# A decoder trunk on one core: weight units loaded, rounded and split in two halves, the low part written over the raw words

## Chip, core and metric

The kernel runs on one core of one Trainium2 chip. Its time is the device time of the whole program, in microseconds (us). The core has a matrix engine (TensorE, PE), whose weight loads stand in a lane of their own (PEld), and VectorE (DVE), ScalarE (ACT), GpSimd (POOL) and SyncE (SP). SP here does little but issue the loads of the weights.

## What is computed

A decoder trunk of two layers on 512 tokens of width 1024, everything in fp32. Cut to what matters, the reference is:

```python
def swiglu(x, w_gate_up, w_down):
    gate, up = jnp.split(x @ w_gate_up, 2, axis=-1)
    return (jax.nn.silu(gate) * up) @ w_down

for l in range(DEPTH):                                   # DEPTH = 2
    h = h + 0.5 * swiglu(rmsnorm(h, ffn1_norm[l]), ffn1_w_gate_up[l], ffn1_w_down[l])
    u = rmsnorm(h, mix_norm[l])
    # layer 0: gated DeltaNet, layer 1: forgetting attention; both beside attention into 256 memory tokens
    h = h + jnp.concatenate([main, mem_out], axis=-1) @ w_out[l]
    h = h + 0.5 * swiglu(rmsnorm(h, ffn2_norm[l]), ffn2_w_gate_up[l], ffn2_w_down[l])
    # after layer 0: shared keys and values from rmsnorm(h) @ kv_w
return rmsnorm(h, final_norm)
```

The hidden width of the feed-forward is 2816, so the four feed-forward blocks hold most of the multiplications.

## The kernel before

**Units.** All weights pass through 189 units. A full unit is 2048 fp32 words for each of the 128 partitions (1 MB): 8 blocks along the contracted dimension by 256 output columns. A unit of a down projection is 1408 words (11 blocks of 128 columns, 704 KB), two of them to one output tile; two units, the first ones of the gdnin and kv phases, have 1024 words. Unit u uses slot u % 2, and a slot holds three tiles: `raw` (as loaded), `w_hi` (rounded to fp32r) and `w_lo` (raw minus w_hi, rounded).

**Steps of a unit.** SP loads `raw` with two DMAs (`load`, line 380, issued at line 383). ACT writes `w_hi` (`round_hi`, line 873, at line 880). DVE writes `w_lo` (`cut_lo`, line 1214, at line 1219). PE then makes three products for each block, hi by x_hi, hi by x_lo and lo by x_hi (`split_products`, lines 464 to 466), so a full unit has 48 matmuls and a down unit 33.

**Waits.** A load of unit u waits until `w_lo` of unit u-2 is cut (semaphore `lo_ready`), which is when `raw` is no longer read. `round_hi` of unit u waits for the load and for `unit_done` of unit u-2, which is when PE has left `w_hi` and `w_lo`. PE waits for `w_lo` of its whole unit (line 472 in `unit`, line 490 in `down_tile`).

**Order on the engines.** Each engine runs its own written order, phase by phase: memtr, xtr, memkv (4 short units of 256 tokens), memvtr, up0, down0, gdnin0, gdn0, wout0, up1, down1, kv0, up2, down2, foxin0, fox0, wout1, up3, down3, final. In an up phase a step is, on ACT: `round_hi` two units ahead, Silu (line 976), then after POOL's product (line 1714) `hid_hi` (line 980); on DVE: the scaled copy out of PSUM (line 1248), `cut_lo` two units ahead, `hid_lo` (line 1359). The second unit of the next down phase waits for the last `hid_lo`. In a down phase step m is, on ACT: `round_hi` of units 2m+2 and 2m+3 of the phase, `feed_hi` (x_hi of the next phase, line 883), a square (line 895); on DVE: `cut_lo(2m+2)`, the update of h (line 1375), `feed_lo` (x_lo, line 1225), `cut_lo(2m+3)`; on POOL: one addition of the square into `square_sum` (line 1695). The units of step m+1 are the ones that `cut_lo` makes in step m. The last step of a down phase so makes the first two units of the next phase. Steps 0 to 5 of the 8 run in a hardware loop, the last two stand by themselves. In down3, the last one, `feed_hi` and `feed_lo` are left out, and DVE makes y_t from h alone.

In gdnin0 and kv0 the first unit has only 24 matmuls, and takes x_hi and x_lo block by block as they come. After it PE sums the squares over the partitions (line 505), for the root mean square of ACT.

Of the kernel before, what the change touches and what calls it, by code (L numbers as in the profile page):

```python
# [2 lines left out]

# [25 lines left out]
P = 128  # L29
# [20 lines left out]
HALF = NP // 2  # L50
FULL_UNIT = KT * 2 * P
DOWN_UNIT = HALF * P
ROW_B = 32


# [42 lines left out]
def build_trunk(nc, mem, x, ffn1_norm, ffn1_gu, ffn1_down, mix_norm, ffn2_norm, ffn2_gu, ffn2_down,  # L98
# [21 lines left out]
    with ExitStack() as ctx:  # L120
# [53 lines left out]
        for s in range(2):  # L174
            slot_at.append(cursor[0])
            raw.append(place(f"raw{s}", [P, FULL_UNIT]))
            w_hi.append(place(f"w_hi{s}", [P, FULL_UNIT], F32R))
            w_lo.append(place(f"w_lo{s}", [P, FULL_UNIT], F32R))
        x_at, X_BYTES = cursor[0], 2 * KT * SEQ * 4
        x_hi = place("x_hi", [P, KT, SEQ], F32R)  # L180
        x_lo = place("x_lo", [P, KT, SEQ], F32R)
# [115 lines left out]
        raw_in = [sem(f"raw_in{s}") for s in range(2)]  # L297
# [71 lines left out]
        def weights_landed(u0, i=0):  # L369

            return 32 * (u0 // 2 + 1) + 32 * i

        block = ctx.enter_context(nc.Block())


        @block.sync
        def _(sp):
            def load(u0, parts, i=0):

                if u0 >= 2:  # L380
                    sp.wait_ge(lo_ready, u0 - 1 + 2 * i)
                for dst, src in parts:
                    sp.dma_start(dst, src).then_inc(raw_in[slot(u0)], 16)

            def load_cols(u0, w, col, i=0, width=2 * P):
                dst = raw[slot(u0)][:, 0:KT * width].rearrange("p (k n) -> p k n", k=KT)
                half = KT // 2
                load(u0, [(dst[:, a:a + half, :], w[:, a:a + half, bass.ds(col, width)])
                          for a in (0, half)], i)

            def load_gate_up(u0, w, n, i=0):
                dst = raw[slot(u0)][:].rearrange("p (k g n) -> p k g n", k=KT, g=2)
                load(u0, [(dst[:, :, g, :], w[:, :, bass.ds(g * FFN + n, P)]) for g in (0, 1)], i)

            def load_down(u0, w, half, n, i=0):
                dst = raw[slot(u0)][:, 0:DOWN_UNIT].rearrange("p (k n) -> p k n", k=HALF)
                cut = HALF // 2
                load(u0, [(dst[:, a:b, :], w[:, half * HALF + a:half * HALF + b, bass.ds(n, P)])
                          for a, b in ((0, cut), (cut, HALF))], i)

            for name in phases:
                kind, idx = name[:-1], int(name[-1])
                u = first_unit[name]
                if kind == "memtr":
                    sp.dma_start(mem_tok[:], mem_rows).then_inc(mem_in, 16)
                elif kind == "memkv":
                    if idx == 0:
                        sp.wait_ge(x_in, 16 * TT)
                    for n in range(2):
                        load_cols(u + n, blocks(mem_w_kv[idx]), n * MEM_WIDTH)  # L410
                elif kind == "up":
                    for n in range(2):
                        load_gate_up(u + n, ffn_gu[idx], n * P)
                    with sp.Fori(0, NP // 2 - 1) as i:
                        for j in range(2):
                            load_gate_up(u + 2 + j, ffn_gu[idx], (2 * i + (2 + j)) * P, i)
                elif kind == "down":
                    with sp.Fori(0, KT) as m:
                        for half in range(2):
                            load_down(u + half, ffn_down[idx], half, m * P, m)  # L420
                elif kind == "gdnin":
                    w = blocks(gdn_w_in[0])
                    dst = raw[slot(u)][:, 0:KT * P].rearrange("p (k n) -> p k n", k=KT)
                    a_col = 4 * WIDTH
                    load(u, [(dst[:, :, 0:ROW_B], w[:, :, a_col:a_col + ROW_B]),
                             (dst[:, :, ROW_B:P], w[:, :, a_col + HEADS:a_col + HEADS + P - ROW_B])])
                    for n in range(12):
                        load_cols(u + 1 + n, w, n * 2 * P)
                    load_cols(u + 13, w, 4 * WIDTH + 2 * HEADS)
                elif kind == "foxin":  # L430
                    for n in range(4):
                        load_cols(u + n, blocks(fox_w_in[0]), n * 2 * P)
                elif kind == "wout":
                    for n in range(KT // 2):
                        if idx == 0 and n == 1:
                            sp.wait_ge(w_prod, TT)
                        load_cols(u + n, blocks(w_out[idx]), n * 2 * P)
                elif kind == "kv":
                    w = blocks(kv_w)
                    dst = raw[slot(u)][:, 0:KT * P].rearrange("p (k n) -> p k n", k=KT)  # L440
                    load(u, [(dst[:, :, 0:HEADS], w[:, :, 2 * WIDTH:2 * WIDTH + HEADS]),
                             (dst[:, :, HEADS:P], w[:, :, 0:P - HEADS])])
# [10 lines left out]
        def _(pe):  # L453
# [14 lines left out]
            def unit(u0, g0, xh, xl, i=0, outs=2, tokens=SEQ, feed=None, ready=x_ready, release=False,  # L468
                     order=range(KT)):

                s, width = slot(u0), outs * P
# [1398 lines left out]
```

## Time and profile before

| | |
|---|---|
| median of 3 runs | 2218.85 us (2218.21 to 2219.61) |
| span of the profiled execution | 2218.7 us |
| PE busy | 2129.1 us, 96% of the span |
| PEld busy | 1743.8 us, 79% |
| DVE busy | 932.8 us, 42% |
| ACT busy | 842.6 us, 38% |
| POOL busy | 429.7 us, 19% |
| DMA | 188.64 MB, 85 GB/s over the span |
| mean granted TensorE clock | 0.979 |

The time of the profiled execution outside its span is not shown apart; the span lies 0.15 us under the median of the unprofiled runs. Busy time of PE counts matmuls from start to modelled end, and these overlap: one 128x512 matmul is shown with 390 ns while the next starts 226 ns after it. So a full unit takes 10.87 us of PE and a down unit 7.48 us at full clock.

### The profile page before, as it was taken

How to read it: one execution, taken by the hardware profiler on the slowest of the kernel's cores; microseconds unless marked ns; L12 is line 12 of the kernel's file. 1: busy time of each engine (PE TensorE's matmuls, PEld its weight loads, DVE VectorE, ACT ScalarE, POOL GpSimd, SP SyncE). 2: the span in 40 equal slices, each digit the busy share in tenths (PEclk: the TensorE clock that was granted, in tenths of full speed). 3: DMA queues.
4: the chain of work that ended last, by engine and by line, in shares of the span. 5: the costliest groups of instructions: out<-in, count | busy, mean ns of one | idle time of the engine just before them, and what ended most of it. 6: DMA issues, size and time to landing. Idle time of an engine off the chain costs nothing.

```text
span 2218.7 us, 25639 instructions
## 1 busy us (share of the span) xinstructions
PE 2129.1 (96%) x9944; PEld 1743.8 (79%) x9944; DVE 932.8 (42%) x864; ACT 842.6 (38%) x939; POOL 429.7 (19%) x288
## 2 busy tenths in 40 slices
PE   6999999999989989999999999999999899999998
PEld 5788888877758878888888888888887478888886
DVE  6433333465442335333333443333434545333333
ACT  4333332367533434344322334432222544344221
POOL 3121210223132612212211011221110012212211
PEclk8999999999999999999999999999998999999999
DMA  4333323322100013433233443332334003333232
GB/s 153 107 100 96 95 71 99 106 76 85 49 1 1 1 53 84 111 95 95 77 102 96 143 124 95 95 95 84 91 109 152 1 22 110 97 95 95 78 93 75
DMA packets 319222, 188.64 MB, mean 85 GB/s; under 512 B 10537, under 2 KB 316858, under 8 KB 318906
## 3 DMA queue, kind: packets, MB, share of 16 engines
q1 hardware_dynamic: 317168, 179.33, 28.2%
q10 hardware_dynamic: 1130, 5.32, 0.6%
q0 software_dynamic: 864, 3.15, 0.3%
q8 instruction: 43, 0.70, 0.1%
q14 instruction: 17, 0.14, 0.0%
HBM read 182.53 MB, written 5.24 MB: 85 GB/s over the span
## 4 chain that ended last, share of the span: by engine, by line
PE 60%; DVE 1%; ACT 1%; issue 0%; ACTq 0%; POOL 0%; DVEq 0%; POOLq 0%
PE ps L464 19%; PE ps L466 19%; PE ps L465 19%; PE ps L849 1%; PE ps L515 0%; PE ps L830 0%; PE ps L541 0%; DVE f_stat L1647 0%; DVE fp L1643 0%; PE ps L818 0%; PE ps L532 0%; PE ps L839 0%; DVE w_lo L1219 0%; ACT bias_ts L1180 0%; PE ps L505 0%
## 5 line engine op out<-in xcount | busy, mean ns | idle before, releaser
L464 PE MATMUL ps<-x_hi,w_hi 128*128 128x512 f32 x1920 | 755.8, 394 | 15.3 <-DVE w_lo L1219 8.6
L465 PE MATMUL ps<-x_lo,w_hi 128*128 128x512 f32 x1920 | 750.1, 391 | 0.0
L466 PE MATMUL ps<-x_hi,w_lo 128*128 128x512 f32 x1920 | 750.1, 391 | 0.0
L880 ACT ACTIVATE w_hi<-raw 128x2048 fp32r<-128x2048 f32 (+2 forms) x189 | 326.3, 1726 | 786.8 <-PE ps L466 755.5
L1219 DVE TENSOR_TENSOR w_lo<-raw,w_hi 128x2048 fp32r<-128x2048 f32 (+2 forms) x189 | 414.4, 2192 | 227.6 <-ACT w_hi L880 227.2
L464 PEld LDWEIGHTS ps<-x_hi,w_hi 128*128 128x128 f32 x1920 | 362.6, 189 | 99.0 <-DVE w_lo L1219 10.8
L465 PEld LDWEIGHTS ps<-x_lo,w_hi 128*128 128x128 f32 x1920 | 362.6, 189 | 77.2 <-issue 1.9
L466 PEld LDWEIGHTS ps<-x_hi,w_lo 128*128 128x128 f32 x1920 | 362.1, 189 | 75.5
L1714 POOL TENSOR_TENSOR gate_up<-gate_up 128x512 f32<-128x512 f32 x88 | 194.5, 2210 | 795.8 <-ACT gate_up L976 795.8
L466 PE MATMUL ps<-hid_hi,w_lo 128*128 128x512 f32 x704 | 273.9, 389 | 0.0
L464 PE MATMUL ps<-hid_hi,w_hi 128*128 128x512 f32 x704 | 273.9, 389 | 0.0
L465 PE MATMUL ps<-hid_lo,w_hi 128*128 128x512 f32 x704 | 273.9, 389 | 0.0
L1248 DVE TENSOR_TENSOR gate_up<-ps,rstd 128x1024 f32<-128x1024 f32 x88 | 107.8, 1225 | 326.8 <-PE ps L466 326.2
L1695 POOL TENSOR_TENSOR square_sum<-square_sum,gate_up 128x512 f32<-128x512 f32 (+1 forms) x64 | 94.4, 1475 | 529.4 <-ACT gate_up L895 483.2
L464 PEld LDWEIGHTS ps<-hid_hi,w_hi 128*128 128x128 f32 x704 | 132.1, 188 | 27.7
L466 PEld LDWEIGHTS ps<-hid_hi,w_lo 128*128 128x128 f32 x704 | 132.1, 188 | 27.4
L465 PEld LDWEIGHTS ps<-hid_lo,w_hi 128*128 128x128 f32 x704 | 132.1, 188 | 27.2
L1359 DVE TENSOR_TENSOR hid_lo<-gate_up,hid_hi 128x512 f32 (+1 forms) x88 | 60.9, 693 | 180.7 <-ACT hid_hi L980 180.7
L980 ACT ACTIVATE hid_hi<-gate_up 128x512 f32 (+1 forms) x88 | 55.8, 634 | 212.0 <-POOL gate_up L1714 212.0
L1375 DVE SCALAR_TENSOR_TENSOR h<-ps,h 128x512 f32 (+1 forms) x32 | 22.1, 692 | 152.0 <-PE ps L466 152.0
L1225 DVE SCALAR_TENSOR_TENSOR x_lo<-h,gains,x_hi 128x512 fp32r<-128x512 f32 (+1 forms) x56 | 44.1, 810 | 38.9 <-ACT x_hi L883 38.9
L895 ACT ACTIVATE gate_up<-h 128x512 f32<-128x512 f32 (+1 forms) x56 | 33.8, 617 | 66.1 <-DVE h L1572 52.2
(256 smaller groups left out, 1570.6 us busy)
## 6 DMA issues: line engine op xcount, KB each, us to landing
raw<-in_ffn_w_gate_up SPq DMA_DIRECT2D x176, 512.0 KB, 4.9
raw<-in_ffn_w_down SPq DMA_DIRECT2D x64, 384.0 KB, 3.9
raw<-in_ffn_w_down SPq DMA_DIRECT2D x64, 320.0 KB, 3.2
raw<-in_gdn_w_in SPq DMA_DIRECT2D x26, 512.0 KB, 4.6
raw<-in_w_out SPq DMA_DIRECT2D x16, 512.0 KB, 4.4
raw<-in_kv_w SPq DMA_DIRECT2D x12, 512.0 KB, 5.0
raw<-in_mem_w_kv SPq DMA_DIRECT2D x8, 512.0 KB, 4.8
raw<-in_fox_w_in SPq DMA_DIRECT2D x8, 512.0 KB, 4.1
```

Source lines behind the costliest of these rows:

```text
L464: nc.tensor.matmul(dst, hi, xh, start=first, stop=False)
L465: nc.tensor.matmul(dst, hi, xl, start=False, stop=False)
L466: return nc.tensor.matmul(dst, lo, xh, start=False, stop=last)
L880: nc.scalar.activation(w_hi[s][:, 0:n], raw[s][:, 0:n], ACT.Copy).then_inc(hi_ready, 1)
L895: nc.scalar.activation(gate_up[:, b, 0, 0:tokens], src, ACT.Square).then_inc(sq_ready, 1)
L980: nc.scalar.activation(hid_hi[:, bass.ds(at, 1), :], gate_up[:, j, 0:1, :], ACT.Copy).then_inc(hid_hi_ready, 1)
L1219: nc.vector.tensor_tensor(w_lo[s][:, 0:n], raw[s][:, 0:n], w_hi[s][:, 0:n].bitcast(F32), ALU.subtract).then_inc(lo_ready, 1)
L1225: nc.vector.scalar_tensor_tensor(dst, src, gain, hi.bitcast(F32), op0=ALU.mult, op1=ALU.subtract).then_inc(x_ready, 1)
L1248: nc.vector.tensor_tensor(dst, src, by, ALU.mult).then_inc(evac, 1)
L1359: nc.vector.tensor_tensor(hid_lo[:, bass.ds(at, 1), :], gate_up[:, j, 0:1, :], hid_hi[:, bass.ds(at, 1), :].bitcast(F32), ALU.subtract).th ...
L1695: nc.gpsimd.tensor_tensor(square_sum[:, 0:tokens], square_sum[:, 0:tokens], gate_up[:, b, 0, 0:tokens], ALU.add).then_inc(sum_ready, 1)
L1714: nc.gpsimd.tensor_tensor(gate_up[:, j, 0, :], gate_up[:, j, 0, :], gate_up[:, j, 1, :], ALU.mult).then_inc(prod_ready, 1)
```

## The change

A unit is handled in two halves, from the load to the matmuls, and `w_lo` lies at the address of `raw`: DVE writes the difference over its own input. The half is cut at 1024 words: blocks 0 to 3 and 4 to 7 of a full unit, blocks 0 to 7 and 8 to 10 of a down unit. A load now needs what PE reads to be free: the first half of unit u waits for `half_used` of unit u-2, which PE raises with the ninth of the 16 (in a down unit: of the 11) split products of that unit; the second half waits for `unit_done` of unit u-2. Four DMAs load a unit instead of two (256 KB each in a full unit; 256, 256, 64 and 128 KB in a down unit). ACT and DVE have two instructions per unit instead of one, and ACT's wait for `unit_done` is gone. PE waits for the first half at the start of a unit, and for the second in the middle. The loads of the two narrow units spread over the whole tile. An SBUF area of 8192 bytes per partition stays as padding, so that the tiles of the other phases lie as before.

```diff
+            w_lo.append(place(f"w_lo{s}", [P, FULL_UNIT], F32R, at=slot_at[s]))
             w_hi.append(place(f"w_hi{s}", [P, FULL_UNIT], F32R))
-            w_lo.append(place(f"w_lo{s}", [P, FULL_UNIT], F32R))
+        cursor[0] += 8192
...
-            def load(u0, parts, i=0):
+            def load(u0, half, parts, i=0):
                 if u0 >= 2:
-                    sp.wait_ge(lo_ready, u0 - 1 + 2 * i)
+                    sp.wait_ge((half_used, unit_done)[half], u0 - 1 + 2 * i)
                 for dst, src in parts:
-                    sp.dma_start(dst, src).then_inc(raw_in[slot(u0)], 16)
+                    sp.dma_start(dst, src).then_inc(raw_in[slot(u0)][half], 16)
...
+                for half, cuts in enumerate(((0, 4, DOWN_CUT), (DOWN_CUT, DOWN_CUT + 1, HALF))):
+                    load(u0, half, [(dst[:, a:b, :], w[:, part * HALF + a:part * HALF + b, bass.ds(n, P)])
+                                    for a, b in zip(cuts, cuts[1:])], i)
...
             def unit(...)
-                pe.wait_ge(lo_ready, u0 + 1 + 2 * i)
+                pe.wait_ge(lo_ready, 2 * u0 + (1 if order == range(KT) else 2) + 4 * i)
                 for i_c, c in enumerate(order):
+                    if i_c == KT // 2 and order == range(KT):
+                        pe.wait_ge(lo_ready, 2 * u0 + 2 + 4 * i)
...
+                        if (c, o) == (KT // 2, 0):
+                            last.then_inc(half_used, 1)
...
             def down_tile(...)
-                    pe.wait_ge(lo_ready, u0 + half + 1 + 4 * i)
+                    pe.wait_ge(lo_ready, 2 * (u0 + half) + 1 + 8 * i)
+                        if c == DOWN_CUT:
+                            pe.wait_ge(lo_ready, 2 * (u0 + half) + 2 + 8 * i)
+                        if c == DOWN_CUT:
+                            last.then_inc(half_used, 1)
...
             def round_hi(u, i=0):
-                    act.wait_ge(raw_in[s], weights_landed(u, i))
-                    if u >= 2:
-                        act.wait_ge(unit_done, u - 1 + 2 * i)
-                    nc.scalar.activation(w_hi[s][:, 0:n], raw[s][:, 0:n], ACT.Copy).then_inc(hi_ready, 1)
+                    for half in range(2):
+                        act.wait_ge(raw_in[s][half], weights_landed(u, i))
+                        nc.scalar.activation(half_of(w_hi[s], n, half), half_of(raw[s], n, half),
+                                             ACT.Copy).then_inc(hi_ready, 1)
...
             def cut_lo(u, i=0):
-                    dve.wait_ge(hi_ready, u + 1 + 2 * i)
-                    nc.vector.tensor_tensor(w_lo[s][:, 0:n], raw[s][:, 0:n],
-                                            w_hi[s][:, 0:n].bitcast(F32), ALU.subtract).then_inc(lo_ready, 1)
+                    for half in range(2):
+                        dve.wait_ge(hi_ready, 2 * u + half + 1 + 4 * i)
+                        nc.vector.tensor_tensor(half_of(w_lo[s], n, half), half_of(raw[s], n, half),
+                                                half_of(w_hi[s], n, half).bitcast(F32),
+                                                ALU.subtract).then_inc(lo_ready, 1)
```

## Rows read from the trace of the kernel before

**Rows 1.** The page, its first part: engine, busy us, share of span, instructions.
```profile
PE 2129.1 (96%) x9944; PEld 1743.8 (79%) x9944; DVE 932.8 (42%) x864; ACT 842.6 (38%) x939; POOL 429.7 (19%) x288
```

**Rows 2.** Waits of PE: line, waited for, us in total, times, longest us.
```profile
PE ps L464 <- DVE w_lo L1219: 8.6, 4, 4.1
...
PE ps L612 <- POOL sq L1763: 2.4, 3, 0.8
```

**Rows 3.** Lines 880 and 1219 by themselves: count, duration ns min/median/max, forms.
```profile
L880 ACT ACTIVATE w_hi<-raw x189: 1060/1915/1921, 18.3 to 2188.4; 128x2048 fp32r<-128x2048 f32 x123, 128x1408 fp32r<-128x1408 f32 x64, 128x1024 fp32r<-128x1024 f32 x2
...
L1219 DVE TENSOR_TENSOR w_lo<-raw,w_hi x189: 1226/2292/3383, 20.3 to 2189.9; 128x2048 fp32r<-128x2048 f32 x123, 128x1408 fp32r<-128x1408 f32 x64, 128x1024 fp32r<-128x1024 f32 x2
```

**Rows 4.** The page, DMA issues: count, KB each, median us from issue to landing.
```profile
raw<-in_ffn_w_down SPq DMA_DIRECT2D x64, 384.0 KB, 3.9
raw<-in_ffn_w_down SPq DMA_DIRECT2D x64, 320.0 KB, 3.2
...
raw<-in_kv_w SPq DMA_DIRECT2D x12, 512.0 KB, 5.0
...
raw<-in_kv_w SPq DMA_DIRECT2D x1, 24.0 KB, 2.3
```

**Rows 5.** Timeline, one looped tile of down1: start us, duration us, what.
```profile
1150.72 0.39 PE L464 MATMUL ps<-hid_hi,w_hi 128*128 128x512 f32 x1
...
1150.92 1.38 ACT L880 ACTIVATE w_hi<-raw 128x1408 fp32r<-128x1408 f32 x1 [6.10 <-PE ps L466]
1152.21 0.70 ACT L883 ACTIVATE x_hi<-h,gains  x1
...
1153.60 1.39 POOL L1695 TENSOR_TENSOR square_sum<-square_sum,gate_up 128x512 f32<-128x512 f32 x1 [13.56 <-ACT gate_up L895]
...
1153.76 2.71 DVE L1219 TENSOR_TENSOR w_lo<-raw,w_hi 128x1408 fp32r<-128x1408 f32 x1
...
1158.20 0.39 PE L464 MATMUL ps<-hid_hi,w_hi 128*128 128x512 f32 x1
```

**Rows 6.** Timeline, step 6 of down0, outside the loop; below, the looped steps.
```profile
417.26 2.79 POOL L1695 TENSOR_TENSOR square_sum<-square_sum,gate_up 128x512 f32<-128x512 f32 x1 [13.64 <-ACT gate_up L895]
...
417.29 1.61 DVE L1219 TENSOR_TENSOR w_lo<-raw,w_hi 128x1408 fp32r<-128x1408 f32 x1
...
L1219 DVE TENSOR_TENSOR w_lo<-raw,w_hi x12: 1624/2170/2718, 318.7 to 402.4; 128x1408 fp32r<-128x1408 f32 x12
```

The last row is line 1219 by itself in the six looped steps of down0, with its columns as in rows 3.

**Rows 7.** Timeline, the end of down1 and the start of kv0.
```profile
1225.53 0.39 PE L464 MATMUL ps<-x_hi,w_hi 128*128 128x512 f32 x1
...
1227.61 0.70 ACT L883 ACTIVATE x_hi<-h,gains 128x512 fp32r<-128x512 f32 x1
...
1229.01 3.38 DVE L1219 TENSOR_TENSOR w_lo<-raw,w_hi 128x2048 fp32r<-128x2048 f32 x1
...
1232.45 0.50 PE L464 MATMUL ps<-x_hi,w_hi 128*128 128x512 f32 x1 [0.47 <-DVE w_lo L1219]
```

**Rows 8.** Timeline in gdnin0 at the start of its unit 3, and the window 462:464.
```profile
462.44 0.80 PE L464 MATMUL ps<-x_hi,w_hi 128*128 128x512 f32 x1 [4.13 <-DVE w_lo L1219]
...
467.30 0.63 PE L466 MATMUL ps<-x_hi,w_lo 128*128 128x512 f32 x1
467.73 0.48 PE L464 MATMUL ps<-x_hi,w_hi 128*128 128x512 f32 x1
...
462.00:464.00 2.00, 1.56 (x4) 1.28 (x5) 2.00 (x4) 1.92 (x3) 0.00 (x0) 0.50 0.28 31
```

In the last row the columns are the window, its length, busy us and count of PE, PEld, DVE, ACT and POOL, the granted clock, the DMA share and GB/s.

**Rows 9.** Timeline, the end of up1 and the second unit of down1.
```profile
1111.00 0.69 DVE L1359 TENSOR_TENSOR hid_lo<-gate_up,hid_hi 128x512 fp32r<-128x512 f32 x1 [1.85 <-ACT hid_hi L980]
...
1113.33 0.39 PE L464 MATMUL ps<-hid_hi,w_hi 128*128 128x512 f32 x1
```

**Rows 10.** Timeline, first rounding of the kernel, and the start of up0.
```profile
18.32 1.91 ACT L880 ACTIVATE w_hi<-raw 128x2048 fp32r<-128x2048 f32 x1 [2.28 <-DMA raw<-in_mem_w_kv]
...
66.09 1.28 DVE L1332 COPY mem_v<-ps 128x512 f32<-128x512 f32 x2
...
66.88 0.77 PE L464 MATMUL ps<-x_hi,w_hi 128*128 128x512 f32 x1 [3.49 <-DVE w_lo L1219]
```

More of the change, by code:

```diff
@@ L52 @@
 DOWN_UNIT = HALF * P
+DOWN_CUT = FULL_UNIT // 2 // P
 ROW_B = 32
@@ L296, in build_trunk @@
         table_tr, tables = sem("table_tr"), sem("tables")
-        raw_in = [sem(f"raw_in{s}") for s in range(2)]
+        raw_in = [[sem(f"raw_in{s}_{half}") for half in range(2)] for s in range(2)]
+        half_used = sem("half_used")
         hi_ready, lo_ready = sem("hi_ready"), sem("lo_ready")
@@ L371, in weights_landed, with half_of @@
             return 32 * (u0 // 2 + 1) + 32 * i
+        def half_of(t, n, half):
+            if n == KT * P:
+                return t[:].rearrange("p (k n) -> p k n", k=KT)[:, half * KT // 2:(half + 1) * KT // 2, 0:P]
+            cut = FULL_UNIT // 2
+            return t[:, half * cut:cut + half * (n - cut)]
         block = ctx.enter_context(nc.Block())
@@ L377, in _, with load_down, load_rows @@
         def _(sp):
-            def load(u0, parts, i=0):
+            def load(u0, half, parts, i=0):
                 if u0 >= 2:
-                    sp.wait_ge(lo_ready, u0 - 1 + 2 * i)
+                    sp.wait_ge((half_used, unit_done)[half], u0 - 1 + 2 * i)
                 for dst, src in parts:
-                    sp.dma_start(dst, src).then_inc(raw_in[slot(u0)], 16)
+                    sp.dma_start(dst, src).then_inc(raw_in[slot(u0)][half], 16)
             def load_cols(u0, w, col, i=0, width=2 * P):
                 dst = raw[slot(u0)][:, 0:KT * width].rearrange("p (k n) -> p k n", k=KT)
-                half = KT // 2
-                load(u0, [(dst[:, a:a + half, :], w[:, a:a + half, bass.ds(col, width)])
-                          for a in (0, half)], i)
+                for half in range(2):
+                    k0 = half * KT // 2
+                    load(u0, half, [(dst[:, k:k + 2, :], w[:, k:k + 2, bass.ds(col, width)]) for k in (k0, k0 + 2)], i)
             def load_gate_up(u0, w, n, i=0):
                 dst = raw[slot(u0)][:].rearrange("p (k g n) -> p k g n", k=KT, g=2)
-                load(u0, [(dst[:, :, g, :], w[:, :, bass.ds(g * FFN + n, P)]) for g in (0, 1)], i)
-            def load_down(u0, w, half, n, i=0):
+                for half in range(2):
+                    ks = slice(half * KT // 2, (half + 1) * KT // 2)
+                    load(u0, half, [(dst[:, ks, g, :], w[:, ks, bass.ds(g * FFN + n, P)]) for g in (0, 1)], i)
+            def load_down(u0, w, part, n, i=0):
                 dst = raw[slot(u0)][:, 0:DOWN_UNIT].rearrange("p (k n) -> p k n", k=HALF)
-                cut = HALF // 2
-                load(u0, [(dst[:, a:b, :], w[:, half * HALF + a:half * HALF + b, bass.ds(n, P)])
-                          for a, b in ((0, cut), (cut, HALF))], i)
+                for half, cuts in enumerate(((0, 4, DOWN_CUT), (DOWN_CUT, DOWN_CUT + 1, HALF))):
+                    load(u0, half, [(dst[:, a:b, :], w[:, part * HALF + a:part * HALF + b, bass.ds(n, P)])
+                                    for a, b in zip(cuts, cuts[1:])], i)
+            def load_rows(u0, parts):
+                for half in range(2):
+                    ks = slice(half * KT // 2, (half + 1) * KT // 2)
+                    load(u0, half, [(dst[:, ks, :], src[:, ks, :]) for dst, src in parts])
             for name in phases:
@@ L422, in _ @@
                     w = blocks(gdn_w_in[0])
-                    dst = raw[slot(u)][:, 0:KT * P].rearrange("p (k n) -> p k n", k=KT)
+                    dst = raw[slot(u)][:].rearrange("p (k n) -> p k n", k=KT)[:, :, 0:P]
                     a_col = 4 * WIDTH
-                    load(u, [(dst[:, :, 0:ROW_B], w[:, :, a_col:a_col + ROW_B]),
-                             (dst[:, :, ROW_B:P], w[:, :, a_col + HEADS:a_col + HEADS + P - ROW_B])])
+                    load_rows(u, [(dst[:, :, 0:ROW_B], w[:, :, a_col:a_col + ROW_B]),
+                                  (dst[:, :, ROW_B:P], w[:, :, a_col + HEADS:a_col + HEADS + P - ROW_B])])
                     for n in range(12):
@@ L439, in _ @@
                     w = blocks(kv_w)
-                    dst = raw[slot(u)][:, 0:KT * P].rearrange("p (k n) -> p k n", k=KT)
-                    load(u, [(dst[:, :, 0:HEADS], w[:, :, 2 * WIDTH:2 * WIDTH + HEADS]),
-                             (dst[:, :, HEADS:P], w[:, :, 0:P - HEADS])])
+                    dst = raw[slot(u)][:].rearrange("p (k n) -> p k n", k=KT)[:, :, 0:P]
+                    load_rows(u, [(dst[:, :, 0:HEADS], w[:, :, 2 * WIDTH:2 * WIDTH + HEADS]),
+                                  (dst[:, :, HEADS:P], w[:, :, 0:P - HEADS])])
                     for n in range(HEADS):
@@ L469, in unit @@
                      order=range(KT)):
-                s, width = slot(u0), outs * P
-                pe.wait_ge(lo_ready, u0 + 1 + 2 * i)
+                s, width = slot(u0), 2 * P
+                pe.wait_ge(lo_ready, 2 * u0 + (1 if order == range(KT) else 2) + 4 * i)
                 bank_free(g0, i)
                 for i_c, c in enumerate(order):
+                    if i_c == KT // 2 and order == range(KT):
+                        pe.wait_ge(lo_ready, 2 * u0 + 2 + 4 * i)
                     if feed is not None:
@@ L876, in round_hi @@
                     n, s = unit_words[u], slot(u)
-                    act.wait_ge(raw_in[s], weights_landed(u, i))
-                    if u >= 2:
-                        act.wait_ge(unit_done, u - 1 + 2 * i)
-                    nc.scalar.activation(w_hi[s][:, 0:n], raw[s][:, 0:n], ACT.Copy).then_inc(hi_ready, 1)
+                    for half in range(2):
+                        act.wait_ge(raw_in[s][half], weights_landed(u, i))
+                        nc.scalar.activation(half_of(w_hi[s], n, half), half_of(raw[s], n, half),
+                                             ACT.Copy).then_inc(hi_ready, 1)
             def feed_hi(dst, src, gain):
@@ L1217, in cut_lo @@
                     n, s = unit_words[u], slot(u)
-                    dve.wait_ge(hi_ready, u + 1 + 2 * i)
-                    nc.vector.tensor_tensor(w_lo[s][:, 0:n], raw[s][:, 0:n],
-                                            w_hi[s][:, 0:n].bitcast(F32), ALU.subtract).then_inc(lo_ready, 1)
+                    for half in range(2):
+                        dve.wait_ge(hi_ready, 2 * u + half + 1 + 4 * i)
+                        nc.vector.tensor_tensor(half_of(w_lo[s], n, half), half_of(raw[s], n, half),
+                                                half_of(w_hi[s], n, half).bitcast(F32),
+                                                ALU.subtract).then_inc(lo_ready, 1)
             def feed_lo(name, dst, src, gain, hi, c, i=0):
```

## The prediction

> **What bounds the kernel now.** Read the page's busy shares first: PE is busy 96% of the span [rows 1]. Then the waits of PE: for the operand that this change touches, w_lo, it waits 8.6 us in all, in four places [rows 2]. The weight pipeline (load, round, cut) is otherwise hidden behind matmuls. So there are at most 8.6 us to win, plus what a low clock behind such a wait costs, and the question is how much of the cover the new waits use up. For that one reads timelines: how long after PE has left a unit the successor in the same slot is ready, against how long PE is busy with the other slot: 10.87 us in an up phase (48 matmuls, one every 0.2265 us), 7.48 us in a down phase (33; 1150.72 to 1158.20 in [rows 5]).
>
> Today the load comes early (it waits for a cut, not for PE), so ACT starts 0.20 us after PE leaves, at 1150.92 against 1150.72 [rows 5]. After the change the transfer itself stands between PE's leaving and ACT's start. That is the cost to follow.
>
> **Steady up phases (88 units): nothing.** Let T be the moment at which the next unit's first matmul starts. `half_used` rises with the 27th of 48 matmuls, so the first half is issued at about T-4.5 and has landed by T-0.5. The second half is issued at T+0.3. Its 512 KB take at most the 5.0 us of the row for such a load [rows 4], so they land by T+5.3. Two instructions of half the size follow, at most 1.06 us on ACT and 1.23 us on DVE (the 1024-word forms, the minimum of each line in [rows 3]): T+7.6 at the latest. PE wants that half at T+10.87+5.4. Silu, product and hid_hi of the step come some 3 us later than now, but only hid_lo of the last step has a near reader. The cover is 8 us; without it each us would cost 88 us. The extra instruction of each engine per unit and PE's extra wait per unit cost nothing here: PE already passes two satisfied waits at each unit's start with the usual spacing, as at 1150.72 [rows 5].
>
> **Steady down phases, the large term.** Take the odd unit 2m+3, which DVE cuts last in step m. T' is the first matmul of the other slot's unit (1150.72), and PE wants the odd unit at T'+7.48 less some hundredths; today it has it at 1153.76+2.71=1156.47, T'+5.75, 1.73 us before 1158.20 [rows 5].
> After: `half_used` rises with matmul 27 of 33, whose end is 7x0.2265-0.39=1.2 us before T', and SP needs some 0.15 us to issue, so T'-1.03. The 512 KB are two DMAs of 256 KB. The nearest rows: 320 KB land 3.2 us after issue, and the 384 KB issued 0.56 us later land 3.9 us after theirs, so 704 KB in 4.45 us [rows 4]. Interpolated by bytes, 512 KB take 3.2+192/384x1.25=3.8 us, landing at T'+2.77. The bounds are 3.2 and 4.45.
> ACT rounds half 0 (1.06) from T'+2.8 and starts half 1 0.97 later, at T'+3.77 (all 704 KB are there at T'+3.4). Half 1, 384 words, holds it 0.43 us more, so feed_hi starts at T'+4.2. Today that is 1152.21, T'+1.49. From feed_hi to the start of w_lo there are 1.55 us today, and the steps between stay: T'+5.75.
> Now w_lo meets POOL's addition, which starts 0.16 us earlier, in this relation to feed_hi today as well. w_lo then takes 2.71 us against 1.61 us in step 6, where POOL's addition is the one that grows, to 2.79 us [rows 5, 6]. So a half that takes 1.23 us alone takes 1.23+1.09=2.32: T'+8.07. PE starts 0.06 us behind the cut (1229.01+3.38 to 1232.45 in [rows 7]), at T'+8.13, so 0.66 late. Restarting costs 0.17 us more: that first matmul holds the engine 0.34 instead of 0.23 us, and the next few are slightly slow. This is 0.83 us a tile, in the looped steps 0 to 5 of down0, down1 and down2: 18x0.83=14.9 us. Step 6 has the cut first and lands 1.1 us earlier: nothing. Down3 has neither feed_hi nor feed_lo before the cut, which gives it over 2 us of room: nothing. The even unit of each tile is cut with nothing before it, at T'+2.8+1.06+1.3=T'+5.1 against 7.48: nothing. With the landing at its bounds the term is 18x0.23 (0.06 of waiting and the restart) to 18x1.5: 4 to 27 us, and 0 if POOL and DVE come in the order of step 6.
>
> The Trainium skill, page "DMA: Bandwidth & Descriptors", section "Anatomy of one DMA", fits a transfer as about 2.0 us plus bytes over 436 GB/s. By that 512 KB take 3.2 us, the lower bound above, and the term is 4 us. The trace is against it where it can be tested: 704 KB in a pair took 4.45 us, not 3.65.
>
> **From down to gdnin0 and kv0.** The last step's order on ACT is round_hi (both halves of the next phase's unit 1), then feed_hi of block 7, and PE wants block 7 in the short unit 0, at T+4.76. T is 1225.53 in kv0, unit 1 starts at 1232.45 and feed_hi at 1227.61 [rows 7]. The unit is now full, so its second half (512 KB) comes last: 1 MB from T-1.03, the second part issued at T+0.3. With 5.0 us for the last DMA of such a pair plus its 0.5 us of later issue [rows 4] it lands at T+4.6. ACT: T+5.65, feed_hi T+5.6 (today T+2.08), feed_lo until T+7.15. PE waits there 2.4 us. w_lo half 0 starts at T+7.07, meets POOL, ends at T+9.4, and unit 1 starts at T+9.45 instead of T+6.92: +2.55 us. In kv0 all of that stays. In gdnin0 the chain goes on to unit 3, where PE waits 4.13 us today for round and cut [rows 8]. Root mean square, POOL's masks and the gate rows push this chain by 3.65 us, and by halves PE gets the first half (2.29+1.92, the medians) minus (1.23+1.06) [rows 3], 1.9 us, sooner: +1.8. Together 4.35. foxin0 has a full unit 0 and needs block 7 only at T+9.5: nothing.
> **Clock.** After the wait of 4.13 us the granted clock is 0.50, the lower of the two levels (1.2 GHz), and the matmuls stay 0.43 us apart until 467.7, 5.3 us at half rate, 2.6 us lost [rows 8]. The wait of 0.47 us in [rows 7] had no such consequence. The two new gaps of 2.4 us (with short ones behind) lie between these rows. I count one of two: 2.6 us, between 0 and 5.2.
>
> **From up to down (4 times).** The last hid_lo ends 1.64 us before its reader [rows 9]. ACT now takes the second half of the down unit, 192 KB in two DMAs from T+0.33, before Silu. It lands between the 2.3 us of 24 KB and the 3.2 us of 320 KB behind its issue at T+0.9 [rows 4], so about T+3.4, and Silu starts some 2.3 us later than today: 0.65 late, 2.6 us in all; less if POOL's product, which today shares the time with a long cut, gets faster. I take 1.0.
>
> **The rest.** up0 needs the bank that the copy of mem_v frees, 66.09 to PE's start at 66.88 [rows 10]. That copy is queued on DVE behind the cut of up0's second unit, whose second half is now issued only as PE leaves memkv: +1.4. The first rounding waits for its DMA [rows 10]; with a first half ready earlier, ACT and DVE are done some 0.8 us sooner: -0.8. In gdnin0's steps ACT waits 0.2 us for the second half, ahead of the squares for which PE waits three times [rows 2]: +0.5.
>
> **Sum.** 14.9+4.35+2.6+1.0+1.4-0.8+0.5=23.95 us on the profiled span of 2218.7, which is 0.15 under the median of the runs; on the median, 2242.8.
>
> **Rivals.**
> (1) No stall in the down loops: the half lands like the 320 KB, or DVE comes ahead of POOL. For it: one row shows the latter order, and 0.6 us is small. Against: the twelve cuts in the loop of down0 have a minimum of 1.62 and a median of 2.17, the mean of the two kinds, so six of them, the odd ones, are long [rows 6]. 23.95-14.9=9: 2228.
> (2) Four DMAs land later than two, or the order on SP holds the first half back. 0.6 us more per tile: 18x0.6=10.8: 2253.6.
> (3) Faster: halves serve PE sooner and nothing comes late. The place is gdnin0's unit 3 (-1.9), the start (-0.8) and the two half-us waits for w_lo at the starts of gdnin0 and kv0 (-1.0): 2215.1. It decides if the second half lands by T+1.5 at the phase ends, so that feed_hi is not held; the shortest landing of any load is 2.3 us [rows 4].
> (4) The new waits are all covered, or gains and losses cancel: 2219 to 2223, if down has no stall and the phase ends lose under 2 us each.
> That the change doesn't do what it says I see no room for: SP's wait is replaced outright.
>
> **How the numbers follow.** Forecast (2232 to 2248) 0.49, (1) 0.21, (2) 0.15, (4) 0.10, (3) 0.05. The range 2223 to 2256 leaves out (3), most of (4) and the far end of (2), under 0.2. Within 0.2% (4.4 us, about what a measurement of this kernel can tell from no change) is (4). Faster 0.05, same 0.10, slower 0.85.
>
> **What would show it.** Among PE's waits for w_lo there should be 18 new ones of 0.6 us in the loops of down0, down1 and down2, none in down3 and none in the up loops; ACT's rounding of an odd first half should start at T'+2.8 with a DMA as its releaser; in kv0 and gdnin0 PE waits some 2.4 us for x_lo. The prediction is wrong if 512 KB land within 3.2 us, if POOL's addition no longer stretches the cut, if in-place cutting changes DVE's speed (1.23 us for 1024 words), or if the clock falls in the down loops.

## The result and the profile after

The changed kernel takes 2237.73 us, the median of 4 runs (2232.9 to 2240.68), where the kernel before takes 2218.6 us on the same chip: a ratio of 1.0081 [1.0067, 1.0096], or 19.1 us more. The profiled execution is the longest of the four, 2240.68 us with a span of 2238.6, 19.9 us over the span before. The forecast was 2242.8, or 24 us more.

The page of the changed kernel, its busy shares first, then parts 4 to 6:

```profile
PE 2132.0 (95%) x9944; PEld 1739.6 (78%) x9944; DVE 965.1 (43%) x1053; ACT 872.6 (39%) x1128; POOL 371.9 (17%) x288
...
PE 55%; DVE 3%; DMA 2%; ACT 1%; issue 1%; SPq 0%; ACTq 0%; DVEq 0%; POOL 0%; POOLq 0%
...
L888 ACT ACTIVATE w_hi<-raw 128x1024 fp32r<-128x1024 f32 (+1 forms) x378 | 357.2, 961 | 858.9 <-DMA raw<-in_ffn_w_gate_up 370.6
...
L1725 POOL TENSOR_TENSOR gate_up<-gate_up 128x512 f32<-128x512 f32 x88 | 134.9, 1532 | 858.1 <-ACT gate_up L985 858.1
...
raw<-in_ffn_w_gate_up SPq DMA_DIRECT2D x352, 256.0 KB, 3.1
...
raw<-in_ffn_w_down SPq DMA_DIRECT2D x64, 128.0 KB, 2.6
...
raw<-in_ffn_w_down SPq DMA_DIRECT2D x64, 64.0 KB, 2.5
```

PE does the same work [rows 1], with 3 us more busy time in a span that is 19.9 us longer: the difference is waiting. In the chain that ended last a DMA now has 2% of the span. ACT's rounding, which waited for PE before [rows 5], now waits for the DMA. The waits of PE (line, waited for, us in total, times, longest):

```profile
PE ps L465 <- DVE w_lo L1229: 14.7, 21, 4.0
...
PE ps L621 <- POOL sq L1774: 7.1, 3, 3.7
...
PE ps L465 <- DVE x_lo L1236: 4.3, 2, 2.4
```

Against [rows 2] there are 21 waits for w_lo and not 4. Of these, 18 short ones, of 0.18 to 0.88 us, lie in the looped steps of down0, down1 and down2, one in each; the other three are the start of up0 (4.0), unit 3 of gdnin0 (3.0) and a new one of 0.57 in gdnin0. The two for x_lo are the starts of gdnin0 (1.96) and kv0 (2.38). The waits for POOL's squares grew from 2.4 to 7.1 us, which the prediction put at half a us. No up loop has a wait for w_lo, nor has down3.

Both kernels have 9944 matmuls in the same order, so the start of the same matmul can be compared in the two traces. This tells where the 20 us arise:

| matmul | before | after | later by |
|---|---|---|---|
| up0, some 12 matmuls in | 72.06 | 72.67 | 0.6 |
| down0, last looped tile | 406.85 | 411.87 | 5.0 |
| gdnin0, later sum of squares | 543.44 | 553.53 | 10.1 |
| down1, first looped tile | 1128.29 | 1138.65 | 10.4 |
| down1, last looped tile | 1203.09 | 1216.11 | 13.0 |
| kv0, soon after unit 1 starts | 1232.79 | 1249.34 | 16.5 |
| down2, last looped tile | 1634.50 | 1655.92 | 21.4 |
| fox0 | 1711.98 | 1731.11 | 19.1 |
| last | 2210.16 | 2230.11 | 20.0 |

The tile of [rows 5] in the changed kernel, from the timeline (start us, duration us, what):

```profile
1146.26 0.39 PE L465 MATMUL ps<-hid_hi,w_hi 128*128 128x512 f32 x1
...
1148.93 1.48 ACT L888 ACTIVATE w_hi<-raw 128x1024 fp32r<-128x1024 f32 x2 [6.49 <-DMA raw<-in_ffn_w_down]
...
1150.31 0.71 ACT L892 ACTIVATE x_hi<-h,gains  x1
...
1151.61 1.47 POOL L1706 TENSOR_TENSOR square_sum<-square_sum,gate_up 128x512 f32<-128x512 f32 x1 [14.10 <-ACT gate_up L904]
...
1151.85 2.78 DVE L1229 TENSOR_TENSOR w_lo<-raw,w_hi 128x1024 fp32r<-128x1024 f32 x2
...
1154.21 0.50 PE L465 MATMUL ps<-hid_hi,w_hi 128*128 128x512 f32 x1 [0.31 <-DVE w_lo L1229]
```

Counted from the first row: ACT starts at T'+2.67 (forecast 2.8), feed_hi at 4.05 (4.2), the cut at 5.59 (5.75), PE at 7.95 (8.13) instead of 7.48.

### The profile page after: what moved, and what is told of

Read it like the earlier page. It is cut to its first block, busy times and chain, and to the rows that moved or that the text cites. A ratio compares the mean times of both kernels' runs of the same rounds, so it can differ in the third digit from the quotient of the medians.

```text
span 2238.6 us, 27053 instructions
## 1 busy us (share of the span) xinstructions
PE 2132.0 (95%) x9944; PEld 1739.6 (78%) x9944; DVE 965.1 (43%) x1053; ACT 872.6 (39%) x1128; POOL 371.9 (17%) x288
## 4 chain that ended last, share of the span: by engine, by line
PE 55%; DVE 3%; DMA 2%; ACT 1%; issue 1%; SPq 0%; ACTq 0%; DVEq 0%; POOL 0%; POOLq 0%
PE ps L465 18%; PE ps L467 17%; PE ps L466 17%; DMA raw<-in_ffn_w_down 2%; DVE w_lo L1229 1%; PE ps L858 1%; ACT w_hi L888 0%; PE ps L839 0%; ACT x_hi L892 0%; PE ps L550 0%; SPq L377 0%; PE ps L524 0%; DVE f_stat L1658 0%; DVE fp L1654 0%; PE ps L827 0%
## 5 line engine op out<-in xcount | busy, mean ns | idle before, releaser
L888 ACT ACTIVATE w_hi<-raw 128x1024 fp32r<-128x1024 f32 (+1 forms) x378 | 357.2, 961 | 858.9 <-DMA raw<-in_ffn_w_gate_up 370.6
L1229 DVE TENSOR_TENSOR w_lo<-raw,w_hi 128x1024 fp32r<-128x1024 f32 (+1 forms) x378 | 454.7, 1220 | 401.9 <-ACT w_hi L888 401.5
L1725 POOL TENSOR_TENSOR gate_up<-gate_up 128x512 f32<-128x512 f32 x88 | 134.9, 1532 | 858.1 <-ACT gate_up L985 858.1
```

The source lines that it names most:

```text
L888: nc.scalar.activation(half_of(w_hi[s], n, half), half_of(raw[s], n, half), ACT.Copy).then_inc(hi_ready, 1)
L1229: nc.vector.tensor_tensor(half_of(w_lo[s], n, half), half_of(raw[s], n, half), half_of(w_hi[s], n, half).bitcast(F32), ALU.subtract).then_ ...
L1725: nc.gpsimd.tensor_tensor(gate_up[:, j, 0, :], gate_up[:, j, 0, :], gate_up[:, j, 1, :], ALU.mult).then_inc(prod_ready, 1)
```

## The experiments

In what follows "the kernel after" is the changed kernel. All times are medians, and ratios are against the kernel before on the same chip: 2219.38 us (19 runs) for the first four kernels, 2220.05 us (30 runs) for the other four. The kernel after was timed beside other runs of the kernel before, of 2218.6 us; so what an edit gives back is told by what it leaves of the loss of 19.1 us. The waits and timelines are of one profiled execution each. The 30 runs of the kernel before lie within 4 us, but the nine or ten runs of a kernel below are 7.5 to 15 us apart, with the overlay and without; why they scatter more stays open.

**w_lo in a place of its own again.** The halves, the four DMAs and two instructions per unit stay. Only the overlay goes, and with it the reason why a load must wait for PE.

```diff
-            w_lo.append(place(f"w_lo{s}", [P, FULL_UNIT], F32R, at=slot_at[s]))
...
+            w_lo.append(place(f"w_lo{s}", [P, FULL_UNIT], F32R))
...
-                    sp.wait_ge((half_used, unit_done)[half], u0 - 1 + 2 * i)
+                    sp.wait_ge(lo_ready, 2 * u0 - 3 + half + 4 * i)
...
+                        if u >= 2:
+                            act.wait_ge((half_used, unit_done)[half], u - 1 + 2 * i)
```

> The change with its low part moved back to a place of its own: still two halves, four DMAs a unit, two instructions a unit on ACT and DVE and PE's wait in the middle, but a load waits for the cut of its half two units before, as early as before the change, and ACT waits for PE. Theory A (the cost is the transfer that now stands between PE's leaving and the rounding): all 18 waits for w_lo in the down loops vanish, PE's waits for x_lo at the starts of gdnin0 and kv0 too, and the time is 2218 us, give or take 3. Rival B (halving costs by itself, by twice as many DMAs, instructions and waits): 2230 us or more stay.

Measured: 2216.14 us (10 runs), 0.9982 [0.9971, 0.9993]. PE's waits in it:

```profile
PE ps L620 <- POOL sq L1775: 5.4, 3, 2.9
...
PE ps L464 <- DVE w_lo L1230: 3.8, 2, 2.0
```

The waits in the down loops and those for x_lo are gone, and so is the whole loss. In its looped tiles ACT starts on the two halves at T'-1.16 and T'+0.26, where the kernel after starts on the first at some T'+2.7. It isn't the doubled number of DMAs and instructions that costs, but the transfer between PE's leaving a half and ACT's rounding. Halving alone is worth 0.1 to 0.3%.

**feed_hi ahead of the second rounding.** The kernel after, with one change in the order of ACT in a down step: what doesn't need the late load goes first.

```diff
-                        for half in range(2):
-                            round_hi_4(u + 2 * m + half + 2, i)
+                        round_hi_4(u + 2 * m + 2, i)
                         square_free(name, m, i)
...
                         square(name, j, m, ...)
+                        round_hi_4(u + 2 * m + 3, i)
```

> The change with one reordering on ACT: in a step of a down phase feed_hi and the square come before the rounding of unit 2m+3, not behind it. The loads stay as late as in the change. Theory A with its chain (landing, two roundings, feed_hi, feed_lo, cut beside POOL's addition): feed_hi and POOL's addition move into the time in which ACT waits for the landing, the cut of an odd first half ends at about T'+5.1 instead of T'+7.9, and the 18 waits (12.2 us by step from trace to trace) and the two for x_lo (4.3 us) vanish; 2218 to 2222 us. If the landing alone were too late, or rival B held, 2230 us or more stay.

Measured: 2218.48 us (10 runs), 0.9996 [0.9985, 1.0008]. The whole loss is gone with the overlay still in place. Its waits, and its timeline in a looped tile of down1 with a late landing:

```profile
PE ps L621 <- POOL sq L1774: 7.0, 3, 3.1
PE ps L465 <- DVE w_lo L1229: 6.6, 2, 4.0
...
1156.78 0.72 ACT L892 ACTIVATE x_hi<-h,gains  x1 [4.59 <-DVE h L1386]
...
1158.19 1.41 POOL L1706 TENSOR_TENSOR square_sum<-square_sum,gate_up 128x512 f32<-128x512 f32 x1 [13.54 <-ACT gate_up L904]
...
1158.67 1.48 ACT L888 ACTIVATE w_hi<-raw 128x1024 fp32r<-128x1024 f32 x2 [0.65 <-DMA raw<-in_ffn_w_down]
...
1159.77 1.70 DVE L1229 TENSOR_TENSOR w_lo<-raw,w_hi 128x1024 fp32r<-128x1024 f32 x2 [1.33 <-ACT w_hi L888]
```

x_hi and the square run, and POOL's addition starts, while the DMA is under way. The cut then waits for the rounding alone, 1.33 us of idle DVE, and takes 1.70 us instead of 2.78, because POOL's addition is over (1159.60) when it starts. In sixteen of the eighteen tiles the load lands sooner (ACT starts between T'+2.6 and T'+2.9), the cut meets the end of POOL's addition, and its first half takes 1.23 to 1.8 us. Even so that half is done by T'+5.75 in all eighteen, and PE wants it at T'+7.48. So the load's lateness hurt through the queue of ACT, not through the weights themselves.

**POOL's addition behind the cut.** To test whether the meeting of DVE and POOL is the part of the delay that puts PE late.

```diff
                         for j in range(2):
+                            if idx < 3:
+                                pool.wait_ge(lo_ready, 2 * (first_unit[name] + 2 * j + 3) + 1 + 8 * i)
                             add_square(name, j, j, i=i)
```

> The change with POOL's addition in down0 to down2 held back until DVE has cut the first half of unit 2m+3 (a wait on lo_ready ahead of it); nothing else moves. If the meeting of cut and addition (1.09 us on the cut) is the step that turns a covered chain into a late one, the cut ends at T'+6.8, PE wants it at T'+7.48, and the 18 waits vanish: about 12 us less than the change, 2226 us, perhaps 1 or 2 more since the addition is then late at the ends of down0 and down1. If the landing is what is late whatever POOL does, the time stays at 2235 to 2238 us.

Measured: 2237.92 us (4 runs), 1.0077 [1.006, 1.0094]. The total was missed by 12 us: nearly the whole loss, 18.5 us, is still there. The place was right, as its waits and its looped tile of down1 show:

```profile
PE ps L514 <- POOL square_sum L1706: 7.2, 3, 3.0
...
PE ps L465 <- DVE w_lo L1229: 5.7, 3, 4.0
...
1148.59 1.68 DVE L1229 TENSOR_TENSOR w_lo<-raw,w_hi 128x1024 fp32r<-128x1024 f32 x2
...
1150.03 1.40 POOL L1706 TENSOR_TENSOR square_sum<-square_sum,gate_up 128x512 f32<-128x512 f32 x1 [13.31 <-DVE w_lo L1229]
```

The 18 waits are gone (3 waits for w_lo are left), the cut takes 1.68 us and not 2.78, and by the starts of the same matmuls the three loops give back 4.4, 3.3 and 5.0 us against the kernel after, which is what they had lost. In the tile of the kernel after shown above the two instructions start within 0.3 us of each other, and 1.1 us of the cut's 2.78 is POOL. The Trainium skill, page "SBUF — State Buffer", section "SBUF: two separate sides", says that the port pair shared by VectorE and GpSimd is an exclusive lock for a VectorE operation with two SBUF inputs beside a GpSimd operation that reads SBUF, and that whichever starts first keeps it for the whole instruction. The traces agree for the looped tiles: the one that starts first has its plain duration (POOL 1.47 beside a cut of 2.78; the cut 1.68 when POOL waits), the other pays. They don't for step 6: in [rows 6] POOL's record starts 0.03 us before that of the cut, and it is POOL that pays, with 2.79 us. So from starts this close the payer can't be told.

Where the 12 us went, by the starts of the same matmuls: 5.8 us lie at the two phase ends. The last addition of a down phase now comes later, PE waits for `square_sum` 7.2 us instead of 3.2, and the granted clock is low for 6.8 us behind each (at 437.7 and 1239.8). Another 6.0 us lie in fox0, where this execution has a low clock for 34.1 us and that of the kernel after for 13.7. No instruction there was changed, and the kernel before has 20.5 us at that place, so this may be chance of the execution. Some 1.3 us come back in gdnin0. But the median of four runs agrees with the profiled one, and how much of the last part the edit causes stays open.

**The first half waits for the whole unit too.** This doubles the suspected cost.

```diff
-                    sp.wait_ge((half_used, unit_done)[half], u0 - 1 + 2 * i)
+                    sp.wait_ge(unit_done, u0 - 1 + 2 * i)
```

> The change with the first half's load waiting for unit_done too, 1.35 us later in a down unit. Theory A says that this goes straight into the waits of the down loops: 18 times 1.35 us more, 24 us, and about 1.3 us at each start of gdnin0 and kv0, so some 2264 us; up phases and down3 stay without a wait. If the landing were not on the chain, nothing or far less would come of it: 2238 to 2245 us.

Measured: 2292.64 us (2 runs), 1.0328 [1.0308, 1.0349]. The waits of PE:

```profile
PE ps L465 <- DVE w_lo L1229: 40.2, 24, 4.8
PE ps L621 <- POOL sq L1774: 10.5, 3, 3.7
...
PE ps L465 <- DVE x_lo L1236: 7.3, 2, 3.7
PE ps L465 <- DVE hid_lo L1370: 6.4, 4, 1.9
```

PE's wait in a looped tile is 0.9 to 1.6 us longer than in the kernel after, some 25 us for 18 of them, as expected. But 2264 us were expected in all, and the kernel is 29 us over that. The rest is in up0, which starts 3.3 us later; in the four ends of an up phase, each with a wait for hid_lo of up to 1.9 us (none in the kernel after); in longer waits at the phase ends; in three waits of some 0.5 us behind the down loops; and in the clock, low for 107 us in all where the kernel after has 71, with four stretches of 3.4 us in or near the down loops. So the cover of the change at "up to down" was thin, 0.7 us between the last hid_lo and its reader: with a load 1.35 us later it is gone.

**The new order in the kernel before.** The same edit of ACT's order as above, made in the kernel before, without halves or overlay.

> The kernel before, with the reordering of e2 (feed_hi and the square ahead of the rounding of unit 2m+3). Theory A: there no chain in the down loops is late, so only the two waits of 0.47 us for w_lo at the starts of gdnin0 and kv0 can go: 1 us less than before, within 0.2%. If the order on ACT were a gain of its own, apart from the late loads, this kernel would gain some 10 us or more.

Measured: 2215.87 us (9 runs), 0.9983 [0.9972, 0.9994]. Of the four waits for w_lo the two of half a us are gone, as expected:

```profile
PE ps L464 <- DVE w_lo L1219: 7.3, 2, 3.8
```

The gain is larger than these 1 us. In the profiled execution the rest lies in stretches that the edit doesn't touch, 1.8 us of it ahead of the first changed instruction, so it is not explained.

**Halves, a place of their own, and the new order** together.

> e1 (halves, w_lo in a place of its own, early loads) with the reordering of e2. e1 has no late chain in the down loops, so the order should add nothing to it: 2216 us, give or take 2. It is the candidate for the fastest form; if halves and order both gain, it lies under 2214 us.

Measured: 2216.15 us (10 runs), 0.9986 [0.9976, 0.9995]. This adds nothing to either alone. Their intervals overlap, so the three can't be told apart: 0.1 to 0.3% under the kernel before, and the fastest forms found.

**The new order in the last step only** (step 7 of a down phase), in the kernel after, to part the phase ends from the loops.

```diff
+                        last_step = m == KT - 1
+                        round_hi_4(u + 2 * m + 2, i)
+                        if not last_step:
+                            round_hi_4(u + 2 * m + 3, i)
...
+                        if last_step:
+                            round_hi_4(u + 2 * m + 3, i)
```

> The change with feed_hi ahead of the rounding only in the last step (m=7) of each down phase; the looped steps stay as they are. Theory A: the 18 waits in the down loops stay (12.2 us from trace to trace), the waits for x_lo at the starts of gdnin0 and kv0 vanish and what came behind them: 2.3 us at gdnin0, 3.5 us at kv0, and in gdnin0 some 3 us by which root mean square, gate rows and the q and k steps ran behind. 2229 to 2231 us. If the phase ends cost only what PE waits there (4.3 us), 2233 us.

Measured: 2230.37 us (10 runs), 1.0045 [1.0031, 1.0058]: 10.3 us over the kernel before, so 8.8 of the 19.1 us go with the phase ends. The waits for w_lo are as in the kernel after, and those for x_lo at the phase starts are gone:

```profile
PE ps L465 <- DVE w_lo L1233: 14.6, 21, 4.4
```

**`half_used` one block sooner in a down unit**, with the eighth product and not the ninth, in the kernel after. (The first half is blocks 0 to 7, so this is safe.)

```diff
-                        if c == DOWN_CUT:
+                        if c == DOWN_CUT - 1:
                             last.then_inc(half_used, 1)
```

> The change with half_used of a down unit raised by the last block of the first half (block 7) instead of the next one (block 8): its load is issued three matmuls, 0.68 us, sooner; all else, POOL's addition beside the cut included, stays. Theory A: PE is 0.47 us late in the loops' tiles with a common landing, so 0.68 us cover it: the 18 waits vanish but for tiles with a slow landing, 10 to 12 us less, 2226 to 2228 us. If the chain started with the second half's load (issued at unit_done, unchanged here), nothing would change: 2235 to 2238 us.

Measured: 2228.81 us (10 runs), 1.004 [1.0028, 1.0052]. That is 1 us over what was expected, and 8.8 us of the loss are left. In the profiled execution a load issued 0.7 us sooner leaves two of the 18 waits, of 0.2 us each:

```profile
PE ps L465 <- DVE w_lo L1229: 7.5, 4, 4.0
...
PE ps L465 <- DVE x_lo L1236: 2.6, 2, 1.3
...
1152.08 1.06 ACT L888 ACTIVATE w_hi<-raw 128x1024 fp32r<-128x1024 f32 x1 [5.57 <-DMA raw<-in_ffn_w_down]
```

The last row is from its timeline in down1: the rounding still starts when the DMA ends, but sooner: at T'+1.82 in this tile, and at some T'+2.0 in most of the 18, where the kernel after has T'+2.7. The waits for x_lo at the phase ends shrink too (1.3 us at most instead of 2.4); the first half is freed sooner there as well. This execution took 2223.49 us, 5.3 under the median of the ten, so what the slower ones wait for isn't shown.

## Why the prediction was right, and where it wasn't

**The down loops: right in mechanism, 2.3 us too dear.** Forecast 18x0.83=14.9 us. Measured by the starts of the same matmuls, the slow restart behind each wait included: 4.3 in down0, 3.3 in down1, 5.1 in down2, together 12.65, or 0.70 a tile. Each link of the sum is in the tile shown above, and the cut beside POOL took 2.78 us where 2.32 was forecast, because both halves are in that row (the first alone is done when PE starts at 1154.21; 1151.85 plus 2.32 is 1154.17). What was mis-sized is the landing, taken by interpolation between 320 and 704 KB: over the 18 tiles ACT starts between T'+2.51 and T'+3.23, in the mean at 2.71 and not 2.8, and PE at 8.03 and not 8.13. The restart costs 0.14 us and not 0.17. Halving a cut doesn't shorten what it pays for POOL: the first half takes 2.31 us beside POOL, 1.1 more than alone, as much as the whole cut pays [rows 5, 6]. Taking the suspected things away confirms it from three sides: an earlier load (2228.81), no meeting with POOL (the waits gone), feed_hi ahead of the load (2218.48). Rivals (1) and (2) fall with it, (3) and (4) with the total.

**kv0: right.** Forecast 2.55 us and, as one of two, a half of 2.6 us for the clock, 3.85. Measured 13.2 to 16.5 late, 3.3 us. The timeline of the kernel after:

```profile
1238.69 0.39 PE L465 MATMUL ps<-x_hi,w_hi 128*128 128x512 f32 x1
...
1243.48 1.06 ACT L888 ACTIVATE w_hi<-raw 128x1024 fp32r<-128x1024 f32 x1 [1.23 <-DMA raw<-in_kv_w]
1244.45 0.70 ACT L892 ACTIVATE x_hi<-h,gains 128x512 fp32r<-128x512 f32 x1
...
1245.85 3.43 DVE L1229 TENSOR_TENSOR w_lo<-raw,w_hi 128x1024 fp32r<-128x1024 f32 x2
1245.99 0.79 PE L465 MATMUL ps<-x_hi,w_hi 128*128 128x512 f32 x1 [2.38 <-DVE x_lo L1236]
...
1248.36 1.14 PE L465 MATMUL ps<-x_hi,w_hi 128*128 128x512 f32 x1
...
1240.00:1260.00 20.00, 17.62 (x70) 13.44 (x70) 11.48 (x10) 12.06 (x14) 1.32 (x1) 0.91 0.39 114
```

The second rounding starts at T+4.79 (forecast 4.6), feed_hi at T+5.76 (5.6), the wait for x_lo is 2.38 us (2.4), and unit 1 starts at T+9.67 (9.45). In the last row (window, busy us and count of PE, PEld, DVE, ACT, POOL, then granted clock) the clock is 0.91: it is at its lower level, 1.2 GHz, for 3.4 us from the end of this wait, and a matmul is shown with 0.79 us instead of 0.39.

**gdnin0: the step that failed.** Forecast 1.8+0.5+1.3=3.6 us, measured 5.0 (5.2 to 10.1 late; 9.9 at the end of gdn0, so 4.7 stay). Its start was right in kind: PE waits for x_lo (1.96 us, forecast 2.4), is 7.3 us late at unit 1, and at unit 3 only 6.2, since the first half of w_lo serves it sooner. The clock behind the wait at unit 3 stays full this time, and by 471.48 it is only 3.75 us behind the kernel before (467.73 in [rows 8]): better than forecast. But PE then meets a chain that has no such gain. The reciprocal ends the root mean square, and starts convolution, squares and POOL's products. From the timeline of the kernel after:

```profile
444.56 3.34 DVE L1252 RECIPROCAL rstd<-rstd 128x512 f32<-128x512 f32 x1
...
468.62 0.50 PE L465 MATMUL ps<-x_hi,w_hi 128*128 128x512 f32 x1 [3.02 <-DVE w_lo L1229]
...
495.43 1.90 POOL L1774 TENSOR_TENSOR sq<-q 128x1024 f32<-128x1024 f32 x1
...
497.38 3.09 PE L621 MATMUL ps<-sq,ones 128*128 128x512 f32 x4 [3.66 <-POOL sq L1774]
```

Before, these were at 436.51, 462.44, 488.08 and 490.03, with a last wait of 0.79 us:

```profile
436.51 3.35 DVE L1241 RECIPROCAL rstd<-rstd 128x512 f32<-128x512 f32 x1 [0.35 <-ACT rstd L899]
...
488.08 1.89 POOL L1763 TENSOR_TENSOR sq<-q 128x1024 f32<-128x1024 f32 x1
...
490.03 1.98 PE L612 MATMUL ps<-sq,ones 128*128 128x512 f32 x4 [0.79 <-POOL sq L1763]
```

The reciprocal is 8.05 us late, POOL's product 7.35, and PE at line 621 also 7.35: it takes over the lateness of POOL, and what it had won at unit 3 becomes a wait of 3.66 us. So of the 5.0 us 2.2 are the lateness of this chain, 1.6 come with the clock, which falls behind that wait for 3.4 us, and 1.1 with the waits for the later squares. In the forecast the squares were given half a us, for short waits of ACT. The error was to credit PE with the 1.9 us that halves save at unit 3, without asking what it waits for next. The kernel with feed_hi first shows it without any late load: against the kernel before, PE's unit 3 is 1.4 us and soon 2.4 us sooner, and at line 621 only 0.2 us, with 7.0 us of waits for POOL's squares in all.

**From up to down: 1.0 forecast, 0.3 measured,** all of it at down0. Silu comes 1.9 us later, 2.6 at down0 (forecast 2.3), but POOL's product behind it takes 1.28 us and not 2.21: no long cut stands in its way. In the mean of all 88 it takes 1532 ns now and took 2210. That was named as the thing that could make it less.

**The start:** +0.6 forecast (1.4-0.8), 0.6 measured, but by other terms: at the end of memkv PE is 0.06 us ahead and not 0.8, then loses 1.6 us at the copies and in up0's first wait, and gets 1.0 back since less work falls into the low clock behind it (until 71.5, before 72.0). The sum was luck. **The clock:** 2.6 forecast at one of two gaps, which is what happened (kv0, not gdnin0). That was a count between two rows and not worked out, so it was luck too. A fall behind line 621 was not foreseen, nor a gain of 2.4 us between the end of down2 and fox0 (1711.98 before), of which 0.8 is lost again in the next wait. The windows of 50 us at the same place, before and after:

```profile
1690.00:1740.00 50.00, 40.49 (x159) 26.72 (x157) 24.27 (x30) 16.87 (x39) 1.60 (x2) 0.83 0.13 43
...
1710.00:1760.00 50.00, 39.49 (x166) 26.21 (x165) 24.30 (x32) 17.22 (x41) 1.60 (x2) 0.90 0.12 38
```

The granted clock there is 0.83 before and 0.90 after, with nothing changed in the code. It differs among the profiled executions of the ten kernels, and none of these runs shows that the change makes it.

**The sum,** by the starts of the same matmuls:

| part | forecast | measured |
|---|---|---|
| start | 0.6 | 0.6 |
| from up to down | 1.0 | 0.3 |
| down loops | 14.9 | 12.65 |
| gdnin0, with gdn0 | 3.6 | 4.7 |
| kv0 | 3.85 | 3.3 |
| fox0 | 0 | -1.6 |
| together | 23.95 | 19.95 |

The two columns part by 4 us in all, and not in one place: gdnin0 was priced too low and most others too high, and fox0 belongs to no term. The profiled execution is the slowest of the four; the medians are 19.1 us apart.

## What to carry to other kernels

A buffer that is laid over an operand makes the next transfer start only when its reader is done, so the transfer stands between the reader and the next in-order instruction. Price it as a place in that engine's queue: list all that stands behind the first instruction that needs the data, and put what doesn't need it ahead. Here one such exchange gave back all of 19 us, and freeing the half 0.7 us sooner gave back about half.

When a chain is made faster at one place, ask what the engine waits for next. A gain at one wait that is followed by a wait for another chain is no gain, and lateness at a phase start can come back some 60 us later through a side chain, as at line 621.

## What the hardware showed that was not expected

- **A load a quarter the size landed only 0.5 us sooner.** From issue to landing 256 KB take a median of 2.9 to 3.1 us, 128 KB 2.6, 64 KB 2.5. The Trainium skill, page "DMA: Bandwidth & Descriptors", section "Anatomy of one DMA", has a fit of 2.0 us plus bytes over 436 GB/s, made on DMAs that GpSimd issues; the loads here, like those to which the prediction applied it, are issued by SP. It would give the 256 KB some 2.6 us, an estimate that the trace exceeds.
- **Short waits left the clock alone, and equal long ones don't act alike.** In the down1 loop, with PE idle for 0.18 to 0.33 us every 15 us, the granted clock is 1.00 (first row below, of the kernel after); so it is in down2, with up to 0.88. Behind a wait of 2.38 us it fell in kv0, behind 1.96 us in gdnin0 it didn't. A wait of 3.02 us at gdnin0's unit 3 left it full in the kernel after (the matmul at 468.62 above, 0.50 us), while the same wait is followed by the lower level for 3.4 us in the kernel that frees the half sooner (second row, 0.80 us). Behind 3.66 us (third row, of the kernel after) it fell for 3.4 us, and behind 4.13 us before, to 0.50 [rows 8].
- **The clock scatters from execution to execution.** A low stretch of the profiled executions lasts 3.4 to 17.1 us, and together they come to between 64 and 107 us, 95 in the kernel before and 71 in the kernel after. In fox0 and wout1, where the change touches little, it is 17 to 38 us. So a difference of some 2 us between two profiled executions says little there, and starts of the same matmul must be compared stage by stage.

```profile
1130.00:1230.00 100.00, 98.55 (x428) 79.65 (x427) 37.06 (x39) 27.11 (x40) 9.31 (x7) 1.00 0.32 94
...
464.21 0.80 PE L465 MATMUL ps<-x_hi,w_hi 128*128 128x512 f32 x1 [3.02 <-DVE w_lo L1229]
...
480.00:514.00 34.00, 29.77 (x115) 21.56 (x114) 20.75 (x24) 22.50 (x23) 8.55 (x4) 0.95 0.24 69
```
